# A fused network kernel on one Trainium2 core: the second mixer's attention and output projection in a new order on three engines

## What the reference computes

```
u, c_q, c_kv, k_rope = split_cols(h @ w_in, ODD_SIZES)
y_c = s5_group(u, ...)        # complex diagonal state space, gelu, y * sigmoid(y @ w_glu + b_glu)
y_d = mla_group(c_q, c_kv, ...)  # 8 heads of 64, softmax over a chunk-causal mask
return concatenate([y_c, y_d]) @ w_out
```

## Time and profile before

| | us |
|---|---|
| median of 3 runs | 3440.29 |
| lowest and highest | 3437.87, 3440.71 |
| the profiled execution's own time | 3438.89 |
| its span in the trace | 3436.80 |
| PE busy, share of the span | 98% |
| DVE, ACT busy | 53%, 38% |
| granted TensorE clock, mean of the span | 0.994 |

### The profile page before, as it was taken

The page is one execution under the profiler, slowest core; times in us unless marked ns, Lnnn a source line. Parts: engine busy times, 40 slices in busy tenths (PEclk is TensorE's granted clock), DMA queues, the critical chain, the costliest instruction groups (busy, mean ns, idle before and its releaser), DMA issues.

```text
span 3436.8 us, 42650 instructions
## 1 busy us (share of the span) xinstructions
PE 3362.2 (98%) x17244; PEld 2791.8 (81%) x17244; DVE 1833.0 (53%) x2984; ACT 1310.9 (38%) x2216; POOL 16.8 (0%) x53
## 2 busy tenths in 40 slices
PE   8999999999998999999999999999999999999998
PEld 7768888888866988898888768888888888788887
DVE  5676884433874644354435357543464336664446
ACT  4443543222564422242224344322242226653233
POOL 0000000000100000000000000000000000000000
PEclk9999999999999999999999999999999999999999
DMA  3103213223301222322232211323222232023245
GB/s 130 62 25 107 74 56 112 97 102 101 96 14 38 92 98 98 104 99 97 94 104 83 103 37 56 106 97 102 100 92 98 98 104 83 32 75 110 92 145 168
DMA packets 92567, 307.80 MB, mean 90 GB/s; under 512 B 16014, under 2 KB 17684, under 8 KB 92372
## 3 DMA queue, kind: packets, MB, share of 16 engines
q1 hardware_dynamic: 89528, 301.31, 26.0%
q10 hardware_dynamic: 2844, 3.77, 0.3%
HBM read 302.95 MB, written 2.10 MB: 89 GB/s over the span
## 4 chain that ended last, share of the span: by engine, by line
PE 88%; DVE 7%; ACT 3%; issue 1%; SPq 0%; DMA 0%; DVEq 0%; ACTq 0%
PE ps L319 25%; PE ps L321 24%; PE ps L320 24%; PE ps L316 13%; DVE WL L307 1%; ACT WH L301 1%; DVE R L709 1%; PE ps L2931 0%; DVE XT L875 0%; DVE XL L884 0%; DVE XT L878 0%; ACT XH L646 0%; ACT od_p L2522 0%; ACT R L644 0%; DVE S L722 0%
## 5 line engine op out<-in xcount | busy, mean ns | idle before, releaser
L319 PE MATMUL ps<-XH,WH 128*128 128x512 f32 (+1 forms) x3200 | 1186.6, 371 | 21.0 <-DVE XL L884 12.3
L321 PE MATMUL ps<-XH,WL 128*128 128x512 f32 (+1 forms) x3200 | 1169.9, 366 | 0.0
L320 PE MATMUL ps<-XL,WH 128*128 128x512 f32 (+1 forms) x3200 | 1169.5, 365 | 0.0
L307 DVE TENSOR_TENSOR WL<-RAW,WH 128x1024 fp32r<-128x1024 f32 x567 | 686.0, 1224 | 314.4 <-ACT WH L301 310.8
L319 PEld LDWEIGHTS ps<-XH,WH 128*128 128x128 f32 x3200 | 605.9, 189 | 127.8 <-DVE XL L884 11.3
L321 PEld LDWEIGHTS ps<-XH,WL 128*128 128x128 f32 x3200 | 605.6, 189 | 97.3
L320 PEld LDWEIGHTS ps<-XL,WH 128*128 128x128 f32 x3200 | 606.3, 189 | 95.6 <-issue 1.9
L301 ACT ACTIVATE WH<-RAW 128x1024 fp32r<-128x1024 f32 x567 | 587.5, 1050 | 142.1 <-DMA RAW<-units 82.3
L319 PE MATMUL ps<-HH,WH 128*128 128x512 f32 (+1 forms) x990 | 362.7, 366 | 0.0
L320 PE MATMUL ps<-HL,WH 128*128 128x512 f32 (+1 forms) x990 | 361.8, 365 | 0.0
L321 PE MATMUL ps<-HH,WL 128*128 128x512 f32 (+1 forms) x990 | 361.7, 365 | 0.0
(11 more groups left out here) (603 smaller groups left out, 3265.5 us busy)
## 6 DMA issues: line engine op xcount, KB each, us to landing
RAW<-units SPq DMA_DIRECT2D x567, 512.0 KB, 3.3
XIN<-in_x ACTq DMA_DIRECT2D x2, 1024.0 KB, 6.1
out<-YT SPq DMA_DIRECT2D x8, 256.0 KB, 3.1
mb_pairf<-constants ACTq DMA_DIRECT2D x1, 512.0 KB
GB<-in_ln_g SPq DMA_DIRECT2D x1, 512.0 KB
GB<-in_ln_b SPq DMA_DIRECT2D x1, 512.0 KB
da_pi<-in_positions ACTq DMA_DIRECT2D x1, 256.0 KB, 3.0
wa_dist<-constants ACTq DMA_DIRECT2D x1, 192.0 KB, 2.3
```

Source lines behind the costliest of these rows:

```text
L307: nc.vector.tensor_tensor(WL[:, u % RING, :], RAW[:, u % RING, :], WH[:, u % RING, :].bitcast(F32), ALU.subtract)\
L319: nc.tensor.matmul(out, wh, xh, start=start, stop=False)
L320: nc.tensor.matmul(out, wh, xl, start=False, stop=False)
L321: return nc.tensor.matmul(out, wl, xh, start=False, stop=stop)
```

## The change

It renames banks so that scores need not wait for the state inputs (banks 2 and 6 trade places; the state inputs now fill banks 3 to 6), and writes out one list per engine in place of the three loops over heads, from the first state output to the fifth output tile. The loops' bodies become functions (`turns`, `values`, `turned_p`, `value_hi`, `value_lo`, `glu_hi`, `glu_lo`), some with steps j given singly. The new `out(m, *ks)` multiplies out some of the k of output tile m, so a tile can be begun and left open in its bank. Each operation is issued as often as before, with the same operands but for the banks.

```diff
...
-    GLN = counts("w0 g0 w1 g1 w2 g2 w3 g3 l0 l1 l2 l3 m0 m1 x0 x1 m2 m3 x2 x3")
-    GAN = counts("y0 y1 y2 s0 t0 s1 t1 y3 s2 t2 s3 t3 h0 h1 h2 h3 z0 z1 x0 x1 z2 z3 x2 x3")
+    GLN = counts("w0 g0 w1 g1 w2 l0 g2 w3 g3 l1 l2 l3 m0 m1 x0 m2 m3 x1 x2 x3")
+    GAN = counts("y0 s0 y1 y2 s1 t0 s2 t1 h0 y3 t2 h1 s3 t3 h2 h3 z0 z1 x0 z2 z3 x1 x2 x3")
+    YCN = counts("y0 y2 y1 y3")
...
-    PB = (0, 1, 6, 7)
-    UQB = ((0, 1), (6, 7), (2, 3))
-    YBANK = (6, 7, 3, 4)
+    PB = (0, 1, 2, 7)
+    UQB = ((0, 1), (2, 7), (6, 3))
+    YBANK = (7, 3, 4, 3)
...
-                        last = mm(ps[:, 2 + q, k * NC:(k + 1) * NC], BT[rows, k, L4 - 1 - j, c * P:(c + 1) * P],
+                        last = mm(ps[:, 3 + q, k * NC:(k + 1) * NC], BT[rows, k, L4 - 1 - j, c * P:(c + 1) * P],
...
             if part == 0:
                 pe.wait_ge(s["x"], c + 1)
+                if c:
+                    pe.wait_ge(s["bu_taken"], 4)
+                if c == 3:
+                    pe.wait_ge(s["ga"], GAN["y1"])
...
-        states_in(3)
-        pe.wait_ge(s["bt_done"], 24)
-        pe.wait_ge(s["q_ev"], 24)
-        states_out(0, 0)
-        states_out(0, 1)
...
                 pe.wait_ge(s["c_in"], 32)
-                pe.wait_ge(s["bu_taken"], 4)
...
-        beside = {0: lambda: states_out(3, 0), 1: lambda: states_out(3, 1), 5: lambda: gate(0), 6: lambda: gate(1)}
-        scores(0)
-        for c in (1, 2):
-            states_out(c, 0)
-            states_out(c, 1)
-        for h in range(NH):
-            if h + 1 < NH:
-                scores(h + 1)
+        def turns(h, *js):
             pe.wait_ge(s["comb"], h + 1)
-            if h == 0:
-                pe.wait_ge(s["ga"], GAN["y1"])
-            for j in range(TT):
+            for j in js:
                 if h or j >= 2:
                     pe.wait_ge(s["pt_ready"], 4 * h + j - 1)
...
-            if h in beside:
-                beside[h]()
-            if h:
-                pe.wait_ge(s["o_hi"], 2 * h)
+
+        def values(h):
+            pe.wait_ge(s["o_hi"], 2 * h) if h else pe.wait_ge(s["ga"], GAN["y0"])
...
+        def out(m, *ks):
+            pe.wait_ge(S["split_ready"], e["no"] + m + 1)
+            for k in ks:
+                ready(k)
+                last = three(ps[:, banks_of(e)[m], :], *w_of(e["no"] + m, k), XHk(k), XLk(k), k == 4, k == 7)
+            if k == 7:
+                last.then_inc(S["unit_done"], 1)
+
+        states_in(3)
+        pe.wait_ge(s["bt_done"], 24)
+        pe.wait_ge(s["q_ev"], 24)
+        states_out(0, 0)
+        scores(0)
+        states_out(0, 1)
+        states_out(2, 0)
+        states_out(2, 1)
+        scores(1)
+        states_out(1, 0)
+        states_out(1, 1)
+        turns(0, 0, 1)
+        scores(2)
+        turns(0, 2, 3)
+        states_out(3, 0)
+        states_out(3, 1)
+        turns(1, 0, 1)
+        scores(3)
+        values(0)
+        turns(1, 2, 3)
+        turns(2, 0, 1)
+        values(1)
+        scores(4)
+        turns(2, 2, 3)
+        turns(3, 0)
+        values(2)
+        turns(3, 1, 2)
+        scores(5)
+        turns(3, 3)
+        gate(0)
+        turns(4, 0)
+        scores(6)
+        turns(4, 1)
+        values(3)
+        turns(4, 2, 3)
+        gate(1)
+        turns(5, 0)
+        scores(7)
+        turns(5, 1)
+        values(4)
+        turns(5, 2)
         pe.wait_ge(s["ga"], GAN["z3"])
-        outproj_pe(pe, b, e, e["no"], ready, XHk, XLk)
+        out(0, 4)
+        turns(5, 3)
+        out(0, 5)
+        turns(6, 0)
+        values(5)
+        turns(6, 1)
+        out(0, 0)
+        turns(6, 2)
+        pe.wait_ge(s["p_ready"], 32)
+        for m in (4, 3, 2):
+            out(m, 4)
+        turns(6, 3)
+        out(3, 5)
+        turns(7, 0, 1)
+        out(0, 1)
+        out(2, 5, 0)
+        turns(7, 2)
+        out(4, 5)
+        values(6)
+        out(3, 0)
+        pe.wait_ge(s["pt_ready"], 31)
+        out(1, 4)
+        turns(7, 3)
+        out(1, 5)
+        out(3, 1)
+        out(0, 6)
+        out(1, 0)
+        out(0, 2)
+        out(1, 1)
+        out(4, 0, 1)
+        values(7)
+        out(0, 3)
+        out(1, 6, 2, 3)
+        out(0, 7)
+        out(1, 7)
+        out(2, 1, 6, 2, 3, 7)
+        out(3, 6, 2, 3, 7)
+        out(4, 6, 2, 3, 7)
+        outproj_pe(pe, b, e, e["no"], ready, XHk, XLk, first=D // P - e["tail"])
...
+            act.wait_ge(s["yc"], YCN[f"y{c}"])
+            act.wait_ge(s["gl"], GLN[f"w{c - 1}"]) if c else act.wait_ge(s["x"], 4)
...
+        def turned_p(h, *js):
+            if h == 0:
+                act.wait_ge(s["x"], 4)
+            elif h == 1:
+                act.wait_ge(s["yc"], YCN["y0"])
+            else:
+                act.wait_ge(s["o_ready"], h - 1)
+            for j in js:
...
+        def value_hi(h):
+            act.wait_ge(s["yc"], YCN["y2"] if h < 4 else YCN["y3"])
+            act.wait_ge(s["o_ready"], h + 1)
...
+        hi_to(act, e["ng"] + 2)
         A(TMPA[:, 0:1], ones[:, 0:1], ACT.Exp)
         y(0)
+        hi_to(act, e["ng"] + 3)
         exps(0)
+        square(0)
+        exps(1)
         y(1)
+        turned_p(0, 0, 1)
         y(2)
-        for h in range(NH):
-            if h >= 2:
-                act.wait_ge(s["o_ready"], h - 1)
...
+        square(1)
+        tanh(0)
+        turned_p(0, 2, 3)
+        exps(2)
+        square(2)
+        tanh(1)
+        glu_hi(0)
+        turned_p(1, 0)
+        y(3)
+        turned_p(1, 1)
+        tanh(2)
+        glu_hi(1)
+        square(3)
+        value_hi(0)
+        turned_p(1, 2, 3)
+        exps(3)
+        turned_p(2, 0)
+        value_hi(1)
+        turned_p(2, 1)
+        tanh(3)
+        turned_p(2, 2, 3)
+        turned_p(3, 0)
+        exps(4)
+        glu_hi(2)
+        glu_hi(3)
+        turned_p(3, 1)
+        hi_to(act, e["ng"] + 5)
+        turned_p(3, 2)
+        hi_to(act, e["ng"] + 6)
+        exps(5)
+        value_hi(2)
+        gate(0)
+        turned_p(3, 3)
+        turned_p(4, 0)
+        gate(1)
+        turned_p(4, 1)
+        hi_to(act, e["ng"] + 7)
+        turned_p(4, 2)
+        value_hi(3)
+        exps(6)
+        out_hi(0)
+        turned_p(4, 3)
+        gate(2)
+        gate(3)
+        turned_p(5, 0, 1)
+        out_hi(1)
+        value_hi(4)
+        turned_p(5, 2, 3)
+        exps(7)
+        turned_p(6, 0)
+        value_hi(5)
+        turned_p(6, 1, 2, 3)
+        out_hi(2)
         hi_to(act, e["no"] + 6)
+        turned_p(7, 0, 1)
+        out_hi(3)
+        turned_p(7, 2)
+        value_hi(6)
+        turned_p(7, 3)
+        value_hi(7)
         b["tail_act"](act, e, e["n1"])
...
+            if between is not None:
+                between()
...
-        for c in range(1, 4):
-            scan(c)
-        maxes(0)
-        weights(0)
-        for h in range(NH):
-            if h + 1 < NH:
-                maxes(h + 1)
-                weights(h + 1)
...
+        scan(1)
+        scan(2)
+        scan(3, lambda: maxes(0))
+        maxes(1)
+        weights(0)
+        w(0)
+        weights(1)
+        maxes(2)
+        g(0)
+        w(1)
+        weights(2)
+        g(1)
+        w(2)
+        glu_lo(0)
+        maxes(3)
+        g(2)
+        value_lo(0)
+        w(3)
+        weights(3)
+        value_lo(1)
+        maxes(4)
+        g(3)
+        glu_lo(1)
+        lo_to(dve, e["ng"] + 1)
+        glu_lo(2)
+        glu_lo(3)
+        maxes(5)
+        lo_to(dve, e["ng"] + 2)
+        weights(4)
+        lo_to(dve, e["ng"] + 3)
+        value_lo(2)
+        weights(5)
+        maxes(6)
+        lo_to(dve, e["ng"] + 5)
+        gate(0)
+        value_lo(3)
+        weights(6)
+        lo_to(dve, e["ng"] + 6)
+        gate(1)
+        maxes(7)
+        value_lo(4)
+        out_lo(0)
+        lo_to(dve, e["ng"] + 7)
+        gate(2)
+        weights(7)
+        gate(3)
+        out_lo(1)
+        value_lo(5)
+        out_lo(2)
+        value_lo(6)
+        out_lo(3)
+        value_lo(7)
         lo_to(dve, e["no"] + 6)
         outproj_dve(dve, b, e, e["no"], finish, tail)
```

More of the change, by code:

```diff
@@ L2525, in y @@
         def y(c):
-            act.wait_ge(s["yc"], c + 1)
+            act.wait_ge(s["yc"], YCN[f"y{c}"])
             own.n["ga"] = GAN[f"y{c}"] - 1
@@ L2530, in square, with glu_hi @@
         def square(c):
+            act.wait_ge(s["gl"], GLN[f"w{c - 1}"]) if c else act.wait_ge(s["x"], 4)
             A(GS[:], U[:, c, :], ACT.Square).then_inc(s["ga"], 1)
+        def glu_hi(c):
+            act.wait_ge(s["yc"], 4)
+            act.wait_ge(s["gl"], GLN[f"g{c}"])
+            A(GH[:, c, :], U[:, c, :], ACT.Copy, scale=0.5).then_inc(s["ga"], 1)
+        def turned_p(h, *js):
[6 more added lines that the diff above has]
+            for j in js:
+                act.wait_ge(s["tr"], 4 * h + j + 1)
+                A(PT[h % 2][:, PTO[j]:PTO[j] + (4 - j) * P], ps[:, 5 + j % 2, 0:(4 - j) * P], ACT.Copy).then_inc(s["pt_ready"], 1)
+        def value_hi(h):
```

(34 more changed lines are left out.)

## The result

| | us |
|---|---|
| before, median of 4 runs (lowest, highest) | 3439.22 (3437.87, 3440.71) |
| after, median of 4 runs (lowest, highest) | 3411.85 (3410.06, 3414.68) |
| ratio, with its 95% interval | 0.9923 [0.9911, 0.9935] |
| after, the profiled execution's own time | 3413.24 |
| its span in the trace | 3411.3 |

Faster by 27.4 us in the medians and by 25.6 in the two profiled executions, where 23.2 was forecast. The median lies 0.95 us under the range.

What follows compares the result with a forecast made beforehand. PE's list bounds the kernel, with 27.5 us overhead in a 131.4 us stretch. Work 103.9, entries 0.8, idle 1.5, restarts 0.6 and slips 1.4 make 108.2, gain 23.2, forecast 3417 us, range 3412.8 to 3426.

Steps and rivals of the forecast that it cites:

- PE's work 103.9: First state output to first tail matmul: PE's pieces sum to 103.9 of 131.36 us and stay unchanged.
- entries: Three-pass groups following a float32 piece: 0.09 us more before the second matmul, in nine more places, 0.8 us.
- The 1.2: Heads' transposes: ten take 1.2 us per head, from seven in 0.93 with a modelled end; eight heads 9.6.
- A: Heads' chain keeps its pace of 9 us per head as ACT's work slips; gain 15, 3425 us; chance 0.15.
- B: Finely cut part, head 1's transposes to values(7): granted clock falls, 3462 us if 45 of 63 us; chance 0.04.
- C: No change: late DVE delivery for heads 1 and 2 and a block at the gates, about 3437 us; chance 0.05.
- The floor is all overhead gone, 3440.3 − 27.5 = 3412.8: Range's lower end: all 27.5 us of the stretch's overhead taken off 3440.3 us.
- the same 27.5: Overhead in the stretch, 131.36 less 103.9 us: waits 16.7, clock 6.3, restarts 4.5.
- I add 1.4 for what slips on ACT: Allowance on the stretch for some 60 hand-overs, half known to 0.2 only: from 106.8 to 108.2 us.
- I added 1.4: Step from profiled execution to median: 1.4 us added to 3415.7, giving 3417.1.
- the 6.3 us booked to the clock: First gate unit, second gate unit and one head's values ran slowly after longer waits: 6.3 us of overhead.
- a walk of this kind: Three engines' lists laid against each other with measured durations from heads to output tiles: PE idle 1.5 us in all.

Runs made afterwards that it cites:

- again: The changed kernel, nothing edited, run five more rounds: 3414.91 us, ratio 0.9928 to the kernel before.
- act_slack: The changed kernel with one more ACT copy of 128 by 1024 (1.08 us) behind head 7's exponentials: 3414.91 us, one execution.
- act_tight: The changed kernel with one more ACT copy (1.04 us) between head 0's value copy and head 1's transposed copies: 3415.36 us, one execution.
- stalls: The changed kernel with twelve standstills of PE, made by GpSimd memsets, in two feed-forward layers: 3452.45 us, one execution.
- banks: The kernel before with only the new bank assignment and the moved wait for `bu_taken`, its loops kept: 3436.98 us, ratio 0.9992.
- late_max: The changed kernel with head 0's maxima behind the whole last scan instead of inside it: 3419.89 us, ratio 0.9939.
- better: The changed kernel with the last state output's second part moved between the transposes of heads 1 and 2, gelu steps later: 3413.93 us, ratio 0.9927.

## Why the prediction was right in its mechanism, and which step failed

**The sum.** PE's work 103.9, less 0.9 since ten transposes cost 1.09 and not 1.2; entries 0.8; waits 1.4; restarts 0.5; the slow first product 0.67: 106.4, and 106.16 measured. The 1.2 had a modelled end in it: the group of seven lasts 0.93, but its next piece starts after 0.76, and that of the group of three after 0.33:
```profile
1005.89 0.93 PE L2352 MATMUL ps<-ident,od_p 128*128 128x128 f32 x7
1006.65 2.32 PE L316 MATMUL ps<-od_k,od_q 100*128 100x512 f32 x8
1008.81 0.49 PE L2352 MATMUL ps<-ident,od_p 128*128 128x128 f32 x3
1009.14 2.58 PE L316 MATMUL ps<-od_u,od_kd 128*128 128x512 f32 x8
```
Before, the same group of three behind its wait took 0.55 (1006.73 to 1007.28), 0.22 more, of which no view lists any as a wait. From before, the 25.2 us are 15.3 of waits, 5.6 of clock, 3.5 of restarts and 1.6 of such delay inside the eight groups of three, less 0.8 for entries; the last two gains share what is left over, and how they divide is an estimate.

**Which part brought what.** Undone one at a time in the new order: early maxima 7.5, output pieces among the heads 5.4. Done alone in the old: banks 0.4, the tanh of the gate in time 6.1. These are not shares of one sum (the two orders differ), but they add to 19; what is left, head 5's wait of 4.5 us with its spell and the small waits of heads 0 to 4, was not undone by itself, and how it divides stays open.

**Rivals.** A (heads keep 9 us each) fell: between 1010 and 1060 PE stands still for 1.3 us for copies, where A wanted over 6. B fell: the finely cut stretch has a granted clock of 0.99, and all that is missing to 1.00 is its first 3.27 us, as `again` shows. The Trainium skill ("TensorE: Matmul & The Clock Gate", "A second HAM failure mode: psum-queue depth-cycling") tells of a bf16 kernel in which cycling through PSUM banks, with micro-idles between groups, made the clock go down and up. By that rule it was at risk here, with some 25 pieces more over the same banks; the traces of this order do not agree (0.99, and 1.00 in `again`), so the measurement decides. C fell with the direction.

**What failed: "The floor is all overhead gone, 3440.3 − 27.5 = 3412.8".** The measured median of 3411.85 lies under this lower end of the range. Three things were wrong in the step.

- It took an overhead read in one execution off a median that stood 1.4 us above that execution. Off the execution's own 3438.89, the same 27.5 gives 3411.4.
- It left nothing for the spread. Nine executions of the changed kernel spread over 7.4 us; the first four happened to have their median at 3411.85, the next five at 3414.91, which the range holds. So it is chance that the median fell under it. Where profiles of one kernel part, it is by slow spells of 1 to 3 us that come in one and not in the other, as near 2130 us above.
- It was no floor even in the profiled execution, since 0.9 of the 103.9 us were no work. 131.36 less 103.0 is 28.4 of overhead, which with the median makes 3411.9 at the lowest.

**The forecast itself was 5.2 us too high, in two halves.** 2.5 in the profiled execution: "I add 1.4 for what slips on ACT" was not needed (`act_slack` shows a whole extra microsecond that costs nothing, `act_tight` a place where it costs all), the transposes were 0.9 less, and the slow first product took 0.7 back; some 0.5 is from outside the stretch, what its slow spells left over. And 2.7 between profile and median: I added 1.4, as the kernel before had it, and the changed one's profiled execution lay 1.4 above its median. The sign of that step is chance.

**Terms mis-sized in the experiments.** A slow spell was priced at 1.7 and was 2.8 after 4.38 us. Its cost does not go by the length of the wait alone: `stalls` has 1.7 after 2.14 us, 1.5 after 3.83 and 2.6 after 4.34. And a spell in front of a later wait is no cost, as `banks` shows, so 1.7 of the 6.3 us booked to the clock could not be won by themselves.

## What to carry to other kernels

Where one engine is full, lay the lists of all engines against each other with measured durations and find who is late at each hand-over; a walk of this kind forecast 0.8, 0.5 and 0.2 us of waiting among sixty hand-overs where 0.77, 0.52 and 0.1 came. It is not always as good: it had 3.6 for the 4.38 of `late_max`, and promised a gain for `better`, which came out longer. Price a wait of the full engine with the restart and the slow spell behind it, and move the earliest producer first, since the delays of `late_max` and `act_tight` were never taken up. Give a range the spread of the executions at its lower end too, and take a piece's cost from start to start, since a modelled end or a wait inside a group makes it look longer.

## What the runs showed of the hardware

- Of the standstills laid into feed-forward layers in `stalls`, none of six from 0.67 to 1.80 us was followed by slow matmuls, all six from 2.14 to 4.34 us were, at a loss of 1.5 to 2.6 us each.
- That is no bound for every place. Just ahead of the stretch stand waits of 1.68 and 1.20 us, and the small products behind the first of them ran at a granted clock of 0.53 in the kernel before and of 1.00 in the changed one, where the first product of the stretch was slow.

The same products ahead of the stretch, before and then changed:
```profile
976.91 0.59 PE L316 MATMUL ps<-od_cmr,od_bm 128*32 128x128 f32 x8 [1.68 <-ACT od_v L2504]
977.15 0.77 PE L316 MATMUL ps<-od_cmi,od_bm 128*32 128x128 f32 x8
```
```profile
977.41 0.45 PE L316 MATMUL ps<-od_cmr,od_bm 128*32 128x128 f32 x8 [1.68 <-ACT od_v L2580]
977.62 0.45 PE L316 MATMUL ps<-od_cmi,od_bm 128*32 128x128 f32 x8
...
980.62 3.90 PE L316 MATMUL ps<-od_u,od_bt 32*128 32x128 f32 x64 [1.20 <-DVE od_t L2845]
```
Before, the small products were slow (0.77) and the wait behind them was used up; after, they were quick (0.45), the wait of 1.20 showed, and the first product of the stretch was slow instead, 3.34 us. The state inputs between took 3.8 us from start to start both times, at a granted clock of 0.99 before and 0.73 after. Eight of the twelve profiles fell the second way, four the first, with the same instructions there but for the banks, and in each of the twelve either the small products or the first one was slow, never both.
